# One layer of a hybrid SSD / gated-delta-rule network on Trainium2: the inverses of two heads in one matrix, a folded query scale, one activation table, an earlier load of the first chunk

## What is computed

```python
kb = kc * bc[..., None]
amat = jnp.where(strict, einsum('bhik,bhjk->bhij', kb, kc) * decay, 0.0)
rhs = concatenate([vc * bc[..., None], kb * exp(gcum)[..., None]], axis=-1)
sol = triangular_solve(eye + amat, rhs, left_side=True, lower=True, unit_diagonal=True)
v_new = u - einsum('bhik,bhkv->bhiv', w, S)
attn = einsum('bhik,bhjk->bhij', qc, kc) * decay
o = einsum(..., qc * exp(gcum)[..., None], S) + einsum(..., attn, v_new)
S = S * exp(last)[..., None, None] + einsum(..., kc * exp(last - gcum)[..., None], v_new)
```

## Time and profile before

| | us |
|---|---|
| median of 3 runs | 3541.09 (3535.12 to 3542.61) |
| the profiled execution | 3537.88 |
| its span | 3536.1 |
| busy: PE, DVE, ACT, POOL | 3148.2, 1559.5, 993.9, 447.4 |
| instructions on PE | 20442 |
| mean granted TensorE clock | 0.934 |

### The profile page before, as it was taken

The page is one execution under the profiler, slowest core; times in us unless marked ns, Lnnn a source line. Parts: engine busy times, 40 slices in busy tenths (PEclk is TensorE's granted clock), DMA queues, the critical chain, the costliest instruction groups (busy, mean ns, idle before and its releaser), DMA issues. The chain is left out here.

```text
span 3536.1 us, 53776 instructions
## 1 busy us (share of the span) xinstructions
PE 3148.2 (89%) x20442; PEld 2962.7 (84%) x20442; DVE 1559.5 (44%) x2031; ACT 993.9 (28%) x1607; POOL 447.4 (13%) x525
## 2 busy tenths in 40 slices
PE   3799999999999698989999488899886999997996
PEld 2799999999999577777778227899876999997996
DVE  5455555401010467777676443455324322333444
ACT  3232323211211244434334201333213211122333
POOL 1000000000000233333333122000000000000000
PEclk7899999999999799999999666899998999998998
DMA  1222222222222422223320522754401112215432
GB/s 70 78 97 85 97 85 97 97 85 97 85 97 75 101 59 60 59 60 85 86 66 16 165 95 77 256 202 154 150 12 63 59 68 72 72 60 198 168 128 94
DMA packets 223765, 338.78 MB, mean 96 GB/s; under 512 B 146296, under 2 KB 159336, under 8 KB 223248
## 3 DMA queue, kind: packets, MB, share of 16 engines
q1 hardware_dynamic: 217344, 311.73, 27.2%
q0 software_dynamic: 6288, 25.25, 2.0%
HBM read 243.72 MB, written 93.22 MB: 95 GB/s over the span
## 5 line engine op out<-in xcount | busy, mean ns | idle before, releaser
L521 PE MATMUL pps<-h_hi,pwh 128*128 128x358 f32 (+1 forms) x2112 | 687.9, 326 | 13.8 <-DVE pwl L586 13.8
L521 PE MATMUL pps<-h_lo,pwh 128*128 128x358 f32 (+1 forms) x2112 | 689.5, 326 | 0.0
L521 PE MATMUL pps<-h_hi,pwl 128*128 128x358 f32 (+1 forms) x2112 | 686.9, 325 | 0.0
L521 PEld LDWEIGHTS pps<-h_hi,pwh 128*128 128x128 f32 x2112 | 397.0, 188 | 13.9 <-issue 13.9
L521 PEld LDWEIGHTS pps<-h_hi,pwl 128*128 128x128 f32 x2112 | 398.5, 189 | 0.0
L521 PEld LDWEIGHTS pps<-h_lo,pwh 128*128 128x128 f32 x2112 | 397.4, 188 | 0.0
L1585 PE MATMUL u_ps<-f_hi,up_wh 128*128 128x358 f32 (+1 forms) x1056 | 344.6, 326 | 21.3 <-DVE up_wl L1577 21.3
L1585 PE MATMUL u_ps<-f_lo,up_wh 128*128 128x358 f32 (+1 forms) x1056 | 345.2, 327 | 0.0
L1585 PE MATMUL u_ps<-f_hi,up_wl 128*128 128x358 f32 (+1 forms) x1056 | 344.0, 326 | 0.0
L586 DVE TENSOR_TENSOR pwl<-pw,pwh 128x1024 fp32r<-128x1024 f32 x88 | 107.8, 1225 | 506.2 <-ACT pwh L534 500.1
L1585 PEld LDWEIGHTS u_ps<-f_hi,up_wh 128*128 128x128 f32 x1056 | 199.0, 188 | 22.3 <-issue 22.3
(11 more groups left out here) (398 smaller groups left out, 5378.7 us busy)
## 6 DMA issues: line engine op xcount, KB each, us to landing
projected<-pO SPq DMA_DIRECT2D x88, 536.0 KB, 2.8
pw<-in_w_in SPq DMA_DIRECT2D x88, 512.0 KB, 3.4
scan_chunk<-projected SPq DMA_DIRECT2D x10, 3744.0 KB, 16.8
merge_w<-in_w_out SPq DMA_DIRECT2D x72, 512.0 KB, 3.3
down_w<-in_w_down SPq DMA_DIRECT2D x48, 704.0 KB, 4.1
up_w<-in_w_up SPq DMA_DIRECT2D x44, 512.0 KB, 4.4
mixed<-scan_chunk SPq DMA_DIRECT2D x10, 1248.0 KB, 6.5
ffn<-uf SPq DMA_DIRECT2D x22, 536.0 KB, 3.0
```

The lines of the kernel that those rows point to most:

```text
L521: ins = pe.matmul(ps[:, 3 * u + n, 0:cn], l[u][:, k, :], r[:, k, c0:c0 + cn], start=(k == 0 and a == 0), stop=(k == KD - 1 and a == 2))
```

## The change

1. **Two heads in one matrix.** In each half of four heads, heads n and n+2 share one 104x104 matrix: the first upper, the second lower, that is, transposed. The product for `AT` swaps its operands for the second (`n % 4 // 2`), a further decay product with the mask `early` and an Exp with scale -1 give the second's decays, VectorE adds the two (`v_C`), and the level masks take both sides of the diagonal. 8 heads become 4 pairs. `D` holds for each pair both factors (`which`: 0 and 1), each in two copies, and the access patterns `both`, `both_half` (the same for blocks of one column) and `late_columns` pick every second block from one copy and the rest from the other. The change of factor 0 needs a different left factor for even and odd blocks: two half products (first in the loop over `half`) with a strided output. ScalarE refills `D` with identities at the end of every round; the copies of `T` are gone.
2. **Query scale.** `o` is no longer multiplied; its norm is taken with the squared factor, and the factor joins the norm's in a 104x8 product.
3. **One table.** `preload_act_table_set` names one set with Ln and Exp in the norms, the gates and the scan.
4. **Early first chunk.** SP issues the load of chunk 0 (and of the first decay sums) in the projection, before the tiles of the kind "sigmoid", once the stores of the first 72 tiles have landed. The scan's start then loads chunk 1 alone.

```diff
+            act.preload_act_table_set("natural_log_exp_and_others")
...
-            stages(sp, body)
+            def load_first(kind):
+                if kind == "sigmoid":
+                    for u in range(2):
+                        sp.wait_ge(stored.sems[u], stored.at(NSCAN // 2 - 1))
+                    sp.dma_start(sel[3 * H:3 * H + 3, :, :], sums[:, 0:C].rearrange("(a h) n -> a h n", a=3)).then_inc(
+                        first_in.sems[0], 16)
+                    sp.dma_start(first[:, :, :], scratch[0:NSCAN, :, 0:C].rearrange("m p n -> p m n")).then_inc(
+                        first_in.sems[0], 16)
+
+            stages(sp, body, load_first)
+            sp.wait_ge(first_in.sems[0], first_in.at(0))
...
+        cd = [buf("chunk0", [P, NSCAN, c])] if running else [chunk0, buf("chunk1", [P, NSCAN, c])]
...
+        dec = buf("dec", [P, 2, 6, c])
+        CW = c if running else P
+        D, X = buf("D", [P, 2, 2, HG // 2, CW]), buf("X", [P, HG // 2, CW])
+        mat = buf("mat", [P, 2, HG // 2, c])
...
+        def both(which, pair, l, m=c):
+
+            w = 1 << l
+            n = CW if w > 16 else c // (2 * w) * 2 * w
+            t = D[0:m, which, 0, pair, 0:CW]
+            step = HG // 2 * CW
+            return bass.AP(tensor=t.tensor, offset=t.offset, ap=[list(t.ap[0]), [2 * w, n // (2 * w)], [step + w, 2], [1, w]])
...
-                def decays(bk, head):
...
                     out = ps[0:c, bk, 0:4 * c]
-                    pe.matmul(out, tab["naccT"][0:3 * H + 3, bass.ds(t * C, c)],
-                              sel[u][0:3 * H + 3, head:head + 4, 0:c], start=True, stop=False)
-                    return pe.matmul(out, con["identb"][0:c, 0:c], late[0:c, 0:4 * c], start=False, stop=True)
+                    pe.matmul(out, tab["naccT"][0:3 * H + 3, bass.ds(t * C, c)], heads, start=True, stop=False)
+                    return pe.matmul(out, con["identb"][0:c, 0:c], hidden[0:c, 0:4 * c], start=False, stop=True)
...
+                    if g == 1:
+                        pe.wait_ge(a_dec.sem, a_dec.at(r, 1))
+                        decays(A[0], sel[u][0:3 * H + 3, HS:H, 0:c].rearrange("p (x y) i -> p x y i", y=4)[:, :, 2:4, :],
+                               early).then_inc(m_segL.sem, 1)
...
+                    four(B[hb], hb, c, lambda n: (kT, kbT)[n % 4 // 2][:, n, :], lambda n: (kbT, kT)[n % 4 // 2][:, n, :]).then_inc(m_G.sem, 1)
...
+                    pe.wait_ge(v_AT.sem, v_AT.at(r, hb + 1))
+                    transpose_bank(pe, ps[:, B[hb], :], [mat[0:c, 0, 2 * hb + n, :] for n in range(2)], c, ident).then_inc(m_T.sem, 1)
...
+                    for pair in range(4):
+                        hb = pair // 2
...
-                            pe.wait_ge(v_qk.sem, v_qk.at(r, hb + 1))
-                            pe.wait_ge(a_T.sem, a_T.at(r, hb + 1))
+                            pe.wait_ge(v_qk.sem, v_qk.at(r))
+                            pe.wait_ge(v_D1.sem, v_D1.at(r, min(pair, 1) + 1))
                         else:
-                            pe.wait_ge(v_T.sem, v_T.at(r, n - 1))
-                            pe.wait_ge(v_TTn.sem, v_TTn.at(r, n - 1))
-                        four(A[hb], hb, c, lambda n: mat[0:c, (l + 1) % 2, n, :], lambda n: T_[0:c, n, :]).then_inc(m_X.sem, 1)
+                            pe.wait_ge(v_T.sem, v_T.at(r, 4 * (l - 1) + pair + 1))
+                            pe.wait_ge(v_TTn.sem, v_TTn.at(r, 4 * (l - 1) + pair + 1))
+                        pe.matmul(ps[0:c, PAIR[pair], 0:width(l)], mat[0:c, (l + 1) % 2, pair, :],
+                                  both(0, pair, l + 1), start=True, stop=True).then_inc(m_X.sem, 1)
                     if l < 3 and not running:
...
-                    for hb in range(2):
-                        pe.wait_ge(a_X.sem, a_X.at(r, 2 * l + hb + 1))
-                        if l < nl - 1:
-                            four(B[hb], hb, c, lambda n: TT_[0:c, n, :], lambda n: X[0:c, n, :]).then_inc(m_dT.sem, 1)
-                        four(A[hb], hb, c, lambda n: X[0:c, n, 0:top(l)], lambda n: TT_[0:c, n, :]).then_inc(m_dTT.sem, 1)
+                    for pair in range(4):
+                        hb, bk = pair // 2, PAIR[pair]
+                        pe.wait_ge(a_X.sem, a_X.at(r, 4 * l + pair + 1))
+                        if l == 0:
+                            pe.wait_ge(v_D2.sem, v_D2.at(r, hb + 1))
+                        m = 64 if end and not running else width(l)
+                        n = n_late(l + 1) if end else width(l)
+                        if end:
...
+                        else:
+                            w = 2 << l
+                            out, x = (ap.rearrange("p (m h j) -> p m h j", h=2, j=w) for ap in (
+                                ps[0:m, bk, P:P + n], X[0:c, pair, 0:n]))
+                            for half in range(2):
+                                pe.matmul(out[:, :, half, :], D[0:c, 1, 1 - half, pair, 0:m], x[:, :, half, :],
+                                          start=True, stop=True)
+                        pe.matmul(ps[0:m, bk, 2 * P:2 * P + n], X[0:c, pair, 0:m],
+                                  late_columns(D[0:c, 1, 1, pair, :], l + 1) if end else both(1, pair, l + 1),
+                                  start=True, stop=True).then_inc(m_dTT.sem, 1)
...
+                    pe.wait_ge(v_T.sem, v_T.at(r))
+                    four(A[hb], hb, P, lambda n: D[0:c, (1, 0)[n % 4 // 2], 1, 2 * (n // 4) + n % 2, 0:c], lambda n: res[0:c, n, :]).then_inc(m_VN.sem, 1)
...
+            act.preload_act_table_set("natural_log_exp_and_others")
...
+                        act.wait_ge(m_segL.sem, m_segL.at(r))
+                        act.activation(dec[0:c, :, 2:4, :], bank(A[0], NHB, c)[0:c].rearrange("p (x y) i -> p x y i", y=2),
+                                       ACT.Exp, scale=-1.0).then_inc(a_decL.sem, 1)
...
-                    act.wait_ge(m_T.sem, m_T.at(r, hb + 1))
-                    copy4(T_[0:c, NHB * hb:NHB * hb + NHB, :], B[hb], a_T, c)
                 for l in range(nl):
-                    for hb in range(2):
...
-                        copy4(X[0:c, NHB * hb:NHB * hb + NHB, :], A[hb], a_X, c)
+                        act.activation(X[0:c, pair, 0:n], ps[0:c, PAIR[pair], 0:n], ACT.Copy).then_inc(a_X.sem, 1)
...
+
+                out = D[0:c, :, :, :, 0:c].rearrange("p a s h i -> p (a s h) i")
+                act.activation(out, bmid(con["ident"][0:c, 0:c], 2 * HG), ACT.Copy).then_inc(a_id.sem, 1)
...
+            dve.memset(D[:, :, :, :, :], 0.0)
...
+                dve.scalar_tensor_tensor(out=be[0:c, 3, :], in0=be[0:c, 1, :], scalar=1.0 / P ** 2, in1=be[0:c, 2, :],
+                                         op0=ALU.mult, op1=ALU.mult).then_inc(v_oqs.sem, 1)
...
+                dve.scalar_tensor_tensor(out=be[0:c, 4, :], in0=rs[0:c, u, 1, :], scalar=float(P) ** -0.5, in1=ors[0:c, :],
+                                         op0=ALU.mult, op1=ALU.mult).then_inc(v_oq.sem, 1)
...
+                    both_heads = AT[0:c, 4 * hb:4 * hb + 2, :]
+                    dve.wait_ge(v_AT.sem, v_AT.at(r, hb + 1))
+                    dve.tensor_tensor(both_heads, both_heads, AT[0:c, 4 * hb + 2:4 * hb + 4, :], ALU.add).then_inc(v_C.sem, 1)
...
-                    normalise(r - 1)
+                    normalise(r - 1, 1 - u)
+                dve.wait_ge(a_id.sem, a_id.at(r))
+                for hb in range(2):
+                    dve.wait_ge(m_T.sem, m_T.at(r, hb + 1))
+                    dve.tensor_tensor(both_half(0, hb), both_half(0, hb), ps[0:c, B[hb], 0:2 * c].rearrange(
+                        "p (h m j) -> p h m j", h=2, j=2), ALU.subtract).then_inc(v_D1.sem, 1)
                 for hb in range(2):
                     dve.wait_ge(p_mat.sem, p_mat.at(r, hb + 1))
-                    dve.tensor_tensor(TT_[0:c, heads(hb), :], bmid(con["ident"][0:c, 0:c], NHB),
-                                              mat[0:c, 0, heads(hb), :], ALU.subtract).then_inc(v_TT.sem, 1)
+                    dve.tensor_tensor(both_half(1, hb), both_half(1, hb), mat[0:c, 0, 2 * hb:2 * hb + 2, :].rearrange(
+                        "p h (m j) -> p h m j", j=2), ALU.subtract).then_inc(v_D2.sem, 1)
...
+                        dve.wait_ge(m_dTT.sem, m_dTT.at(r, 4 * l + pair + 1))
+                        for which, done, start in ((0, v_T, v_D1), (1, v_TTn, v_D2)):
...
+                            change = ps[0:m, PAIR[pair], P * (1 + which):P * (1 + which) + n]
...
+                                to = both(which, pair, l + 1, m)
+                                change = change.rearrange("p (m h j) -> p m h j", h=2, j=w)
+                            dve.tensor_tensor(to, to, change, ALU.subtract).then_inc(done.sem, 1)
...
-                dve.tensor_scalar(rs[0:c, u, 1, :], rs[0:c, u, 1, :], float(P) ** -0.5, None, ALU.mult).then_inc(v_rq.sem, 1)
-                dve.wait_ge(v_rq.sem, v_rq.at(r))
-                dve.wait_ge(v_o2.sem, v_o2.at(r))
```

(9 more changed lines are left out.)

180 lines of the change are left out of this document (98 added, 82 removed).

## The result

| | us |
|---|---|
| before, median of 4 | 3541.38 |
| after, median of 4 runs | 3500.79 (3492.4 to 3506.12) |
| after / before | 0.9887 (95% interval 0.9863 to 0.991) |
| the profiled execution after, and its span | 3498.91, 3496.8 |
| busy: PE, DVE, ACT, POOL | 3115.4, 1561.2, 915.5, 374.4 |

The change makes the kernel 1.1% faster, 40.6 us, where 84 were forecast: the sign is right, the size is half, and the time lies above the range. The last line of the table is the first hint: fewer instructions, and a lower clock.

A forecast was written before the change was run, and what follows sets the result against it. It took the scan as bound by TensorE, VectorE right behind. Rounds -61.4, first chunk -11.2, stall +4, tables -10, mask casts +0.6, scan's end -1.9, running sequences -4.3 made -84.2, so 3457 us, range 3420 to 3492.

The forecast's parts named there:

- What bounds the kernel: Scan rounds: bound by TensorE with VectorE right behind; 78.3 us a round at a granted clock of 0.97.
- The levels: Levels 0 to 5 of each scan round: fewer TensorE instructions at 0.092 us each save 5.6 us together.
- The head: VectorE's chain at each round's head: added and removed work nets -0.6 us, bounds 0 and -1.6.
- The tiny products: Small new VectorE products in each round's head, priced at about 0.4 us together.
- A round: One scan round: levels -5.6 and head -0.6 sum to -6.2 us, -61.4 in ten rounds.
- First chunk: Start of the scan: the earlier chunk load saves 11.2 us, a table load included.
- stall: Projection: TensorE stands 4 us for tile 74's weights behind the chunk's transfer, from 0 to 10.
- tables: Norms and gates: eight felt table loads go, saving 10 us, uncertain by 5 in both directions.
- (a): Rival for levels and head: VectorE does not bind the levels, 2.8 us a round more saved, 3429 us; chance 0.12.
- (b): Rival for levels 0 to 4: half products with strided output cost double, 73 us in all, 3530 us; chance 0.08.
- (c): Rival for levels 0 to 4: all strided products cost double, 146 us in all, about 3603 us; chance 0.05.
- (d): Rival for the levels: TensorE's freed time is idle, so levels give nothing, 3513 us; chance 0.05.

The follow-up runs named there:

- early_alone: The kernel before with only the early first chunk (part 4) added; 3523.14 us, ratio 0.9949.
- fill_head: The changed kernel plus 12 unused identity products where TensorE stands in each round's head; 3482.36 us, ratio 0.9841.
- query_alone: The kernel before with only the query scale (part 2) added; 3546.29 us, ratio 1.0017.
- rest_filled: The kernel before with parts 2, 3 and 4, without the pairs, plus filler products in the head and 64-column query sizes; 3498.11 us, ratio 0.9877.
- wide_and_res: The changed kernel with fillers in the head and before the product with the inverse, 64-column query sizes, full-width first half product; 3446.44 us, ratio 0.9732.
- head_wide: fill_head with the first half product of levels 0 to 4 contiguous over all 104 columns; 3463.88 us, ratio 0.9795.

## Why the prediction was wrong, point by point

**What bounds the kernel: right, but read for one state of the clock.** The working took the products' prices at 0.092 us, which is their price at 2.4 GHz, for the whole round and after the change too. The page showed 0.97 and a short stretch at 0.68, and the prediction named the latter without asking what TensorE did before it: stand in the head. **This is the step that failed.** Each term that took work or a transpose from TensorE also changed what it does in between, and the sum had no term for that. Measured, the time at 1.2 GHz rose from 5.5 to 18 us a round.

How much of the miss is this step can be read from one round, the first of the eight, in two kernels that both hold the clock in it. early_alone has the rounds of the kernel before:

```profile
1263.45:1339.45 76.00, 68.86 (x608) 60.22 (x608) 55.29 (x99) 32.59 (x63) 26.87 (x24) 1.00 0.30 69
```

and fill_head the changed ones, with 24 instructions of filler:

```profile
1256.77:1327.33 70.56, 62.53 (x542) 54.67 (x542) 55.21 (x130) 27.43 (x71) 19.64 (x23) 1.00 0.33 74
```

The change takes 5.4 us from this round, where 6.2 were forecast and 1.4 came out in the mean of the plain kernels. Over eight rounds 38 us of the forecast are missing (49.6 less 11.4): an estimate from these rows puts 6 on terms of the wrong size and 32 on the clock.

**The levels: right.** Forecast 2.2 for levels 0 to 2, measured 3 x 0.73 = 2.2 (8.93 to 8.20). Level 3: forecast 1.47, measured 1.63. Level 4: forecast 1.03, measured 0.69 at the full clock (5.89 to 5.20) and +0.59 in the changed kernel, since its clock falls there. Level 5: forecast 0.9, measured 0.72 to the product against the state (3.25 to 2.53). Together 5.2 of the forecast 5.6 at the full clock. The clock in those rows is held by the wide sizes and the fillers, which add up to 0.1 to level 4.

**The head: not the gain that was forecast.** The terms that the prediction lists (-1.23, +1.1, +0.4, -0.7, +0.5) add up to +0.1; the -0.6 that it nets has no row behind the rest. From the norm's product to L1323 it was 5.25 us and is 5.37 (1486.95 to 1492.32), but the additions and most small steps lie ahead of that product: from the scaled keys on VectorE takes 13.21 us before and 14.64 after (1319.70 to 1334.34). The tiny products were priced at 0.4 together; L1355, L1358 and L1362 take 0.57, 0.97 and 0.15 us in the changed kernel, where 0.57 (L1282) stood before. The query's product was no gain to be seen: it lay beside TensorE's work in the tail, and query_alone puts part 2 at +5 to +6 us, the clock's part in it included. The prediction listed the later transposes as a cost of 0.5; they came earlier, for they wait for GpSimd's cut only, and that moved most of TensorE's standing into one piece. In the round at a held clock above, 0.2 us is left for all this beside the 5.2 of the levels.

**A round**: forecast -6.2; at a held clock -5.4 (one round, above), or 5.4 to 5.7 for the pairs alone (rest_filled to wide_and_res); in the changed kernel -1.4.

**First chunk, stall, tables: right.** -11.0 against -11.2, +1.8 against +4, and the two later norms and the gates close to their terms. The stall is smaller since the weights came with the end of the chunk: they were split at 976.03, 17.1 us after the chunk's issue at 958.95, no more than the 17.9 of the earlier trace rows, where the forecast had put the weights' own transfer behind the chunk's. The three norms and the gates together gave 10.7 against 9.4. How many loads were felt no run counts, so the sum doesn't decide between 1283 ns a load and the further drain that the Trainium skill ("ScalarE: Activation LUTs", What ACT_TABLE_LOAD costs) adds to each; the rows do. In the first norm of the kernel before an activation ends at 32.19, a load runs from 32.20 to 33.48, and the next activation starts at 33.50: no drain is seen on either side. Not foreseen, and not explained by a run, are the +3.4 us in the output projections.

**The rivals.** (a) VectorE not binding the levels: refuted, TensorE waits for L1427 in each of levels 0 to 2 (0.72 us in levels 1 and 2 of the round shown). (b) and (c), strided output and input: refuted by 0.092 us an instruction, and head_wide, whose first half product is contiguous, has no cheaper level. The rule of the Trainium skill ("Advanced Engine Details and Errata", PSUM Cachelines) that stood behind (b) is not seen at these shapes, whose runs are of two values and more. (d), the freed time is idle: right for X in levels 0 to 2, as the forecast had it, and it is near what happened in a way that the rival did not have: not idle time, but time at half the clock.

## What to carry to other kernels

Before a change that takes work from TensorE is priced, look at the granted clock in short windows, and at what the engine does ahead of each fall; then ask of the change where it lengthens a stand or leaves products of few columns, and price the work behind it at either level. Removing work from an engine that is not on the path at that point (the product of 1.23 us in the tail) brought nothing here, and with the small dependent steps that paid for it the kernel got 5 to 6 us slower (query_alone). When a change gives less than it should, compare the rounds at a held clock first: a few products into an unused bank, in time in which TensorE stands, separate the two causes in one run.
